# A fused two-block transformer kernel: additions first, scans and reciprocals split, weight parts brought forward in the hand-written order

## The reference

```
x = x + parallel_mixer(rms_norm(x), ...)          # convolution beside a gated linear recurrence (HGRN), 4 heads
x = x + memory_cross_attention(rms_norm(x), rms_norm(mem), ...)   # 4 heads, 256 memory rows, softmax
x = x + hierarchical_moe(rms_norm(x), ...)        # best of 4 groups, best 2 of its 4 experts
h = x + (sigmoid(g_a) * (y_a @ proj_a) + sigmoid(g_b) * (y_b @ proj_b)) @ w_out   # second block
out = h + square(relu(rmsnorm(h) @ w_mlp_in)) @ w_mlp_out
```

## Time and profile before

| | |
|---|---|
| median of 3 runs | 1277.94 us (1276.66 to 1278.69) |
| the profiled execution | 1287.07 us, of which the span of its instructions is 1285.3 us |
| TensorE busy | 1222.2 us, 95% |
| VectorE busy | 909.5 us, 71% |
| ScalarE busy | 722.6 us, 56% |
| GpSimd busy | 116.3 us, 9% |
| mean granted TensorE clock | 0.977 of full speed |
| read from HBM | 253.15 MB, 198 GB/s over the span |

### The profile page before, as it was taken

One profiled execution on the slowest core, in us unless ns is written; L12 is line 12 of the kernel. 1 busy time (PEld: TensorE's weight loads), 2 busy tenths in 40 slices (PEclk: granted clock), 3 DMA queues, 4 the chain that ended last, 5 costly groups with the idle time before them and its releaser, 6 DMA issues. The chain is left out here.

```text
span 1285.3 us, 18841 instructions
## 1 busy us (share of the span) xinstructions
PE 1222.2 (95%) x7850; PEld 1084.2 (84%) x7850; DVE 909.5 (71%) x967; ACT 722.6 (56%) x838; POOL 116.3 (9%) x135
## 2 busy tenths in 40 slices
PE   6999999988999999999999899999989899899998
PEld 5988997977888787887877779999889898889997
DVE  5997677446778878788888885668746955554553
ACT  5745323444477667676766455577767734444442
POOL 0100000000000000000000100038713410000000
PEclk9999999888999999999999899989999999899999
DMA  6433325314489888897987246522234456355552
GB/s 267 158 131 132 132 99 184 132 56 190 147 326 370 321 325 342 300 373 278 361 328 291 104 167 238 186 97 86 94 114 168 131 144 209 116 187 179 191 196 98
DMA packets 38179, 255.43 MB, mean 199 GB/s; under 512 B 4192, under 2 KB 6368, under 8 KB 10320
## 3 DMA queue, kind: packets, MB, share of 16 engines
q1 hardware_dynamic: 34800, 247.64, 53.5%
q10 hardware_dynamic: 3296, 6.61, 1.5%
HBM read 253.15 MB, written 1.08 MB: 198 GB/s over the span
## 5 line engine op out<-in xcount | busy, mean ns | idle before, releaser
L433 PE MATMUL bank<-r,r 128*128 128x512 f32 (+5 forms) x2016 | 673.9, 334 | 36.9 <-DVE r L1734 15.3
L1734 DVE TENSOR_TENSOR r<-f,r 128x2048 fp32r<-128x2048 f32 (+3 forms) x240 | 542.8, 2267 | 195.2 <-ACT r L1175 194.6
L434 PE MATMUL bank<-r,r 128*128 128x512 f32 (+5 forms) x2016 | 663.0, 329 | 0.0
L435 PE MATMUL bank<-r,r 128*128 128x512 f32 (+5 forms) x2016 | 662.8, 329 | 0.0
L1175 ACT ACTIVATE r<-f 128x2048 fp32r<-128x2048 f32 (+3 forms) x240 | 453.4, 1891 | 184.1 <-PE bank L435 164.2
L433 PEld LDWEIGHTS bank<-r,r 128*128 128x128 f32 (+4 forms) x2016 | 380.2, 189 | 82.3 <-issue 34.4
L435 PEld LDWEIGHTS bank<-r,r 128*128 128x128 f32 (+4 forms) x2016 | 381.5, 189 | 35.1
L434 PEld LDWEIGHTS bank<-r,r 128*128 128x128 f32 (+4 forms) x2016 | 380.3, 189 | 34.7 <-issue 1.0
L1743 DVE TENSOR_TENSOR r<-f,r 128x512 fp32r<-128x512 f32 (+3 forms) x70 | 54.8, 788 | 31.4 <-ACT r L1701 11.2
L2517 POOL TENSOR_SCALAR f<-f,f 128x128 f32<-128x128 f32 (+1 forms) x64 | 64.5, 1025 | 43.9 <-DVE f L2312 43.9
L443 PE MATMUL bank<-f,f 128*128 128x128 f32 x224 | 33.1, 309 | 8.8 <-DMA f<-in_cst 6.3
(11 more groups left out here) (314 smaller groups left out, 987.7 us busy)
## 6 DMA issues: line engine op xcount, KB each, us to landing
f<-in_weights SPq DMA_DIRECT2D x216, 1024.0 KB, 4.9
f<-in_weights SPq DMA_DIRECT2D x12, 896.0 KB, 4.6
f<-in_weights SPq DMA_DIRECT2D x8, 672.0 KB, 4.6
f<-in_weights SPq DMA_DIRECT2D x4, 882.0 KB, 5.4
f<-bias_table ACTq DMA_DIRECT2D x1, 2048.0 KB, 13.5
f<-in_mem ACTq DMA_DIRECT2D x1, 1024.0 KB, 4.8
out<-f ACTq DMA_DIRECT2D x2, 512.0 KB, 2.6
f<-in_moe ACTq DMA_DIRECT2D x1, 647.0 KB, 3.7
```

The source lines that it names most:

```text
L433: e.matmul(o, lh.r, rh.r, start=start, stop=False)
L434: e.matmul(o, lh.r, rl.r, start=False, stop=False)
L435: return e.matmul(o, ll.r, rh.r, start=False, stop=stop)
L1734: e.tensor_tensor(slot_of(n).r, slot_of(n).f, high_of(n).r.bitcast(F32), ALU.subtract).then_inc(s["w_lo"], 1)
```

## The change

On TensorE a new function `proj_turned` does the first projection after five of the normalisings: for each of the eight blocks it takes both halves of the outputs. The dense expert's gate does the same over four quarters, with the routing logits between. `scatter` goes through the columns first. The bank rotation differs in the last two attention pairs and at the start of the feed-forward network. On VectorE and ScalarE calls stand in another order: all four additions come ahead of the normalising; the first unit's low part is made in two halves, the third's right after the second's, and the softplus of the RG-LRU (an Exp and an Ln) stands behind the logarithm of the HGRN gates; the reciprocals are made in halves; in cross-attention the maximum of head h+1 stands ahead of the division of head h; the routing matrices (`tiles`) stand one unit's low part sooner; additions of a tile's outcome stand between low parts; a tile's outcome is cut as soon as each half is there; scans of the RG-LRU have a unit's low part between them.

```
@@ -457,7 +457,31 @@
             def wait_turn(q, part=4):
                 e.wait_ge(s["n_lo"], 4 * q + part)
 
-            def proj_t(name, j, c, nk, M, src, evac, turned=None):
+            def proj_turned(name, q, src, evac):
+
+                key = (name, 0)
+                n = at[key]
+                let_go()
+                b = take(key)
+                if n:
+                    e.wait_ge(s["w_lo"], n + 1)
+                else:
+                    e.wait_ge(s["w_lo0"], 1)
+                wh, wl = high_of(n).re("p (k f) -> p k f", k=8), slot_of(n).re("p (k f) -> p k f", k=8)
+                for k in range(8):
+                    if k % 2 == 0:
+                        wait_turn(q, k // 2 + 1)
+                    if n == 0 and k == 4:
+                        e.wait_ge(s["w_lo"], 1)
+                    for c in range(2):
+                        o, f = banks[b][:, c * 256:c * 256 + 256], slice(128 * c, 128 * c + 128)
+                        e.matmul(o, wh.r[:, k, f], src[1].r[:, k, :], start=k == 0 and c == 0, stop=False, skip_group_check=True)
+                        e.matmul(o, wh.r[:, k, f], src[0].r[:, k, :], start=False, stop=False, skip_group_check=True)
...
@@ -531,8 +553,7 @@
                 e.wait_ge(s[f"l_x{a // 2}"], 16)
                 turn(0, a)
             scale_row(0)
-            proj_t("hf", 0, 0, 8, 128, XTT, "ev_a", turned=0)
...
@@ -661,9 +681,10 @@
                 e.wait_ge(s["x_add"], a + 1)
                 turn(2, a)
             scale_row(2)
-            for j in range(4):
+            proj_turned("q", 2, XTT, "ev_a")
+            for j in range(1, 4):
                 for c in range(2):
-                    proj_t("q", j, c, 8, 128, XTT, "ev_a", turned=2 if (j, c) == (0, 0) else None)
...
                     wh, wl = high_of(n).re("p (k f) -> p k f", k=4), slot_of(n).re("p (k f) -> p k f", k=4)
-                    for fb in range(4):
-                        if (name, u, fb) == ("gate", 0, 2):
-                            turn_logits()
-                        o, f = banks[bs[fb // 2]][:, (fb % 2) * 256:(fb % 2) * 256 + 256], slice(fb * 128, (fb + 1) * 128)
-                        for kk in range(4):
-                            k = 4 * u + kk
+                    for kk in range(4):
+                        k = 4 * u + kk
+                        if name == "gate" and u == 0:
+                            logits(kk)
+                        for fb in range(4):
+                            o, f = banks[bs[fb // 2]][:, (fb % 2) * 256:(fb % 2) * 256 + 256], slice(fb * 128, (fb + 1) * 128)
                             e.matmul(o, wh.r[:, kk, f], XH.r[:, k, :], start=fb % 2 == 0 and k == 0, stop=False, skip_group_check=True)
                             e.matmul(o, wh.r[:, kk, f], XT.r[:, k, :], start=False, stop=False, skip_group_check=True)
                             m = e.matmul(o, wl.r[:, kk, f], XH.r[:, k, :], start=False, stop=k == 7, skip_group_check=True)
...
                                     first and k == 0, last_x and k == 3)
+                        if last_x and u == 1 and a == 0:
+                            full["dn", g] = done(m)
                     m.then_inc(s["w_used"], 1)
 
...
                 let_go()
-                for i in range(2):
-                    for h in range(2):
+                for h in range(2):
+                    for i in range(2):
...
@@ -1052,12 +1085,14 @@
 
             first = rotation[1]
             for p in range(10):
-                rotation[1] = first if p < 8 else first + 4
+                rotation[1] = first if p < 8 else first + 10 - p
                 if p < 8:
                     scores(p)
                 name, j = ATT_FILL[p]
                 for u in range(2):
                     proj_t(name, j, u, 8, 112 if name == "ur" else 128, XTT, "ev_a")
+                    if u == 0:
+                        rotation[1] = first + 5
                     if 1 <= p < 9:
                         turn_p(2 * p - 2 + u)
...
             acc = [take(("acc", a)) for a in range(4)]
-            rotation[0], rotation[1] = [b for b in range(8) if b not in acc], 0
+            rotation[0], rotation[1] = [(acc[3] + 1 + b) % 8 for b in range(4)], 0
...
             e.activation(lbx[:, 1:3, :], lbx[:, 1:3, :], ACT.Exp).then_inc(s["sv_a"], 1)
-            e.wait_ge(s["sv_d"], 2)
-            k = own(e.activation(sp2[:, 1, :], sp2[:, 1, :], ACT.Exp))
-            e.wait_ge(s["c_act"], k)
-            e.activation(sp2[:, 1, :], sp2[:, 1, :], ACT.Ln, bias=1.0).then_inc(s["sv_a"], 1)
             for p in range(2):
-                ahead(("hf", p))
+                if p:
+                    ahead(("hf", p))
                 wait_unit(("hf", p))
                 o = banks[bank_at["hf", p]][:, :].rearrange("p (j t) -> p j t", j=2)
                 e.activation(HF[pair(p)], o, ACT.Sigmoid)
                 read_out(("hf", p), e.activation(KK[pair(p)], o, ACT.Sigmoid, scale=-1.0))
             e.wait_ge(s["hg_f"], 1)
             e.activation(HF[:, :, :], HF[:, :, :], ACT.Ln).then_inc(s["hg_ln"], 1)
+            e.wait_ge(s["sv_d"], 2)
+            k = own(e.activation(sp2[:, 1, :], sp2[:, 1, :], ACT.Exp))
+            e.wait_ge(s["c_act"], k)
+            e.activation(sp2[:, 1, :], sp2[:, 1, :], ACT.Ln, bias=1.0).then_inc(s["sv_a"], 1)
             for p in range(2):
                 ahead(("hq", p))
...
             def outcome_high(g):
-                wait_unit(("down", 2 * last_of(g) + 1))
                 if g:
                     e.wait_ge(s["pe_done"], full["add", 2 + g, 3])
                 for h in range(2):
+                    if h == 0:
+                        e.wait_ge(s["pe_done"], full["dn", g])
+                    else:
+                        wait_unit(("down", 2 * last_of(g) + 1))
                     e.activation(YEH.r[:, h, :], banks[bank_at["dn", g, h]][:, :], ACT.Copy).then_inc(s["y_h"], 1)
...
                     yb_high(2 * p - 16)
+                    fill_out(*ATT_FILL[p])
                     yb_high(2 * p - 15)
-                    fill_out(*ATT_FILL[p])
 
 
...
             lru_root(0)
             lru_root(1)
+            ahead(("gb", 2))
             lru_gates(2)
-            ahead(("gb", 2))
             k0 = lru_tanh(2)
             gb_out(2)
...
                 low_of(dst[pair(p)], dst_high[pair(p)]).then_inc(s["n_lo"], 1)
 
-            def normalise(q):
+            def first_low(part):
+
+                f = slice(1024 * part, 1024 * part + 1024)
+                m = e.tensor_tensor(slot_of(0)[:, f].r, slot_of(0)[:, f].f, high_of(0)[:, f].r.bitcast(F32), ALU.subtract)
+                m.then_inc(s["w_lo0" if part == 0 else "w_lo"], 1)
+
+            def normalise(q, between=None):
                 scaled(q, 0)
                 scaled(q, 1)
                 turn_low(q, 0)
+                if between is not None:
+                    between()
                 scaled(q, 2)
                 turn_low(q, 1)
...
@@ -1780,13 +1831,13 @@
 
             def add_and_turn(call, last, q, scale=None):
 
-                for a in range(4):
-                    add_back(call, last, scale, [a])
-                    if a:
-                        spread_gain(q, a - 1)
+                add_back(call, last, scale)
+                spread_gain(q, 0)
+                spread_gain(q, 1)
                 diagonal(q, 0)
+                spread_gain(q, 2)
+                diagonal(q, 1)
                 spread_gain(q, 3)
-                diagonal(q, 1)
                 normalise(q)
 
...
             diagonal(0, 1)
-            low(0)
-            normalise(0)
+            e.wait_ge(s["w_hi"], 1)
+            first_low(0)
+            normalise(0, lambda: first_low(1))
             low(1)
+            ahead(("hf", 0))
             e.wait_ge(s["l_cb"], 16)
             e.wait_ge(s["l_sb"], 16)
...
@@ -1953,8 +2005,16 @@
                 e.wait_ge(s["pe_done"], full["os", i])
                 e.tensor_scalar(RS[half(i)], banks[bank_at["os", i]][:, :].rearrange("p (h t) -> p h t", h=4), 1.0 / 128, EPS,
                                 ALU.mult, ALU.add).then_inc(s["os_v"], 1)
+                if i == 1:
+                    inverse_of_half(1, 0)
+                    inverse_of_half(1, 1)
+
+            def inverse_of_half(i, part):
                 e.wait_ge(s["os_v"], i + 1)
-                e.reciprocal(RS[half(i)], RS[half(i)]).then_inc(s["os_r"], 1)
+                cut = (slice(None), slice(2 * part, 2 * part + 2), slice(128 * i, 128 * i + 128))
+                m = e.reciprocal(RS[cut], RS[cut])
+                if part == 1:
+                    m.then_inc(s["os_r"], 1)
 
             def scale_half(i):
...
@@ -2003,16 +2066,25 @@
 
             for j in range(4):
                 ahead(("q", j))
-            for h in range(4):
+            def most(h):
                 a = slice(2 * h, 2 * h + 2)
                 e.wait_ge(s["pe_done"], full["xs", h])
```

(21 more changed lines are left out.)

192 lines of the change are left out of this document (129 added, 63 removed).

## The result

The changed kernel takes **1247.2 us** (median of 6, 1245.7 to 1255.27) where the kernel before took 1278.71 us beside it: ratio 0.9763, 95% interval 0.9737 to 0.979. That is 31.5 us less; 25.2 were forecast, and the time lies 1.2 us above the lower end of the range. The profiled execution took 1246.87 us, its span 1245.1 us, its mean clock 0.992 (before: 0.977).

What follows compares the result with a forecast made beforehand. TensorE, busy 95% of the span, was taken as the bound, its waits mostly ended by VectorE. Ten terms summed to −25.2 us, taking the median from 1277.94 to 1253, own range 1248 to 1259, stated range 1246 to 1266.

Steps and rivals of the forecast that it cites:

- more clock than counted: Rival: shorter waits no longer drop TensorE's clock, −7 us more, −32 in all, 1246; chance 0.12.
- Start: Up to the first HGRN round: low parts sooner, but the moved softplus adds 3.0 us on ScalarE; +0.8 us.
- Tile boundaries: Expert tiles: four waits of 1.42 us for a low part lose 1.15 each; −4.6 us.
- Attention: Attention projections: bank waits of 0.94 and 2.94 us go, plus 1.0 for clock; −4.9 us.
- Feed-forward start: Wait of 4.34 us: 2.0 off by the new bank rotation, 1.2 by the additions; −3.2 us.
- Normalisings: Second and expert normalisings: with all four additions first, the scale comes sooner; −1.2 us each.
- Cross-attention: Maximum a head ahead: 3.3 of 4.16 us of waits before transposes go, plus 1.3 for clock; −4.6 us.
- End of the experts: Wait of 2.29 us at `scatter`: −1.7, a later low part +0.5, additions in quarters −0.3; −1.5 us.
- HGRN reciprocals: Wait of 2.18 us behind a reciprocal: made in halves, scaling begins sooner; −0.9 us.
- RG-LRU: Low parts between scans: wait of 1.96 us goes, that of 3.98 falls to about 2.3; −3.6 us.
- full lock: Rival: at the scans GpSimd and VectorE block each other, 2.3 us late instead of 1.0, twice; 1255.3, chance 0.03.
- The rival of going to and fro: Rival: changing output region in the new loops costs up to 36.3 us over 336 matmuls; 1289, chance 0.03.

Runs made afterwards that it cites:

- e4: The changed kernel with the RG-LRU softplus moved later, among the high parts of the output weights; 1243.81 us, ratio 0.9700 to the kernel before.
- e10: The changed kernel with the four additions of a tile's outcome in one place again, ahead of the hidden values; ratio 0.9774 to the kernel before.
- e7: The changed kernel with the old bank rotation and order of reads in the last two attention pairs; ratio 0.9791 to the kernel before.
- e11: The kernel before, with only the four quarters of the addition put ahead of the normalising steps at three places; 1273.22 us, ratio 0.9944.
- e2: The changed kernel with the quarters of the addition between the normalising steps again, at three places; ratio 0.9794 to the kernel before.
- e6: The changed kernel with the first projection after five normalisings finishing one half of its outputs, then the other, as before; ratio 0.9758 to the kernel before.
- e8: The changed kernel with the softplus late and a low part moved behind the normalising at the end of the experts; ratio 0.9729 to the kernel before.
- e12: The changed kernel with the softplus late and a low part ahead of a gating behind the scans; 1244.56 us, ratio 0.9716 to the kernel before.

## Why the prediction was right, and where its steps were not

The direction, the size and most places came as argued; the sum was 6 us short, and the rival named "more clock than counted" (−32, 1246), to which I had given 0.12, came nearer than the forecast. That the time still lies in the range, 1.2 us from its end, is owed to that rival, which set the end.

- **Start, +0.8: right** in the stage's length, and the 3.0 us on ScalarE were its cause (e4). The first two waits came as said (3.79 to 2.72, 2.37 gone), but 0.60 and 1.59 stand new behind them. The first score with a wait started at 77.08; I had said 76.9. Other executions begin up to 1 us sooner, so its size is known to about that.
- **Tile boundaries, −4.6: right.** 4 × 1.20 (e10).
- **Attention, −4.9: right in its waits** (3.9, e7), short of its clock (3.4 for 1.0; 1.7 of it in e7's profile behind the second wait).
- **Feed-forward start, −3.2: right in its waits** (3.1). The new rotation is worth its 2.0: the wait is 4.43 in e11, with the additions first and the rotation of before, and 2.33 in e2, the other way round. The stage shrank by 8.9: 3.0 is half clock, and 2.4 is the pace of matmuls, told below, which is not the change's doing.
- **Normalisings, −1.2 each: right in their waits** (1.1 and 1.0), and wrong in that I counted nothing for the clock, 2.9 and 2.7 between the two profiles. The step that failed stands in the rivals: "waits near that length remain". They did remain, at 2.41, and in the changed kernel's profile the clock stayed up behind them, without the 0.49 and 0.64 in front of each. That is a tendency and no rule: with the small waits the half clock stands at 8 of 9 such places, without them at 15 of 33, and e11, where they alone are gone, still has it at all three. What else decides stays open. The other reason that I gave, that the first projection then needs its pairs half as fast, brought nothing (e6).
- **Cross-attention, −4.6:** 2.7 of waits for 3.3, and 2.4 of clock for 1.3.
- **End of the experts, −1.5: wrong.** The wait at the scattering shrank by 1.72, as I had it, but 1.54 came back in front of L443 for the low part that now stood between cut and addition (0.77 stood there before); I had charged 0.5 for it. With the 2.38 behind it grown to 2.70, tiles and end together lost 5.1 of idle time, 4.8 of them at the tile boundaries: some −0.3 is left for the end. e8 shows that it could not be had cheaply: VectorE has no room behind it.
- **HGRN reciprocals, −0.9:** the wait fell by 1.60, and 1.56 stands new at 189.16 behind VectorE's L2040. About −0.3. No run takes this part back alone.
- **RG-LRU, −3.6: too much.** 3.98 became 1.54 and 1.96 became 0.60, but 1.68 stands new behind them: 2.1 in all. Of the 1.68, 1.05 is the low part's 2.80 instead of 1.75 behind GpSimd's product. I had read the 3.26 against 2.29 as a price for company that speaks against a full lock. It was the full lock, as the row beside it would have told (the kernel before, timeline of GpSimd):

```profile
994.03 1.84 POOL L2537 TENSOR_TENSOR f<-f,f 112x768 f32<-112x768 f32 x1 [1.21 <-DVE f L2371]
995.84 3.89 POOL L2525 TENSOR_TENSOR f<-f,f 112x768 f32<-112x768 f32 x1
```

  The first ends at 995.87, 1.10 us after the low part began at 994.77, and the low part was 1.0 longer than alone. The second took 3.89 and ended 1.70 after the low part's end at 998.03. I weighed the lock by its longest case, and not by how much of the other instruction was left.
- **The rival of going to and fro: ruled out** (e6, and the pace above). Its arithmetic was also too high: 336 matmuls change the region 112 times, so one more matmul for each change would be 12.1 us and not 36.3.
- **The rows at half clock:** the profile of before has eleven stretches and not nine, and 52.0 us of work in them and not 41.8, so the clock was undercounted before it was weighed.

The terms for idle time sum to 22.9 and gave 20.4; those for clock sum to 2.3 and gave about 12 over many executions. That one size is the main error. A more careful reader could have had it from the page of before: at a clock of 0.977 some 26 us are lost, most of them behind the very waits that the change shortens.

**The best version** is e4, the changed kernel with the softplus moved once more: 0.9700 of before. Its traces show 3 us less than the changed kernel's, the ratios of e4 and e12 5 to 7. As plain medians, 1243.81 and 1244.56 against 1247.2 and 1249.13, it is 3 to 5, so 3 us are shown and the rest is open.

## What to carry to other kernels

Price a wait at a busy TensorE twice: its own length, and half of the busy time at half clock behind it, times how often that stretch is there; and count the small waits beside the long one, since here they went with more and longer such stretches. Two or three executions do not tell the clock's share, and medians of six can differ by 4 us for it alone, so price single parts by idle time in the trace. When an instruction is moved out of the way on an engine that is full, ask which later wait will pay for it.

## What the runs showed of the hardware that was not expected

- **Two paces of the same matmuls.** In the feed-forward stage the first profile of before has a mean of 281 ns for the matmuls of 256 columns (start to start 0.118 us), the second, of the same kernel, 276 ns (0.113):

```profile
L435 PE MATMUL bank<-r,r 128*128 128x256 f32 x237 | 66.6, 281 | 0.0
```

```profile
L435 PE MATMUL bank<-r,r 128*128 128x256 f32 x229 | 63.2, 276 | 0.0
```

  Both at full granted clock. Over that stage it is about 3 us. e10 ran at the slow pace too, all other profiles at the quick one for at least seven tenths of these matmuls in the stage. Within one execution the pace changes from one run of matmuls to the next, and then holds. The changed kernel's queries ran at 0.113 in its first profile and at 0.118 in its second. What chooses it stays open.
- **The half clock is not a property of a kernel.** Nearly all waits of one kernel agree to 0.1 us between executions (in all, from 0.1 us up, 59.0 and 59.6 before, 38.7 and 38.6 after), the stretches at half clock behind them do not: behind the first projection of the experts there is none in the first profile of the changed kernel, and one of 3.41 us in its second.
- **A GpSimd product behind a VectorE operation with two inputs from SBUF** took 3.8 us instead of 1.85, and the other way round a low part took 2.80 or 3.40 instead of 1.75, and a scan 1.98 instead of 0.66 (above).
